# V rows of an expert lookup gathered six quarter units behind its U rows in place of eight

## The reference

```python
def peer_ffn(h, w_q, sub_keys, u_tab, v_tab):
    ...
    expert = ia * PEER_NKEYS + ib          # 8 heads x 16 experts for each token
    gate = jax.nn.softmax(best, axis=-1)
    ...
        act = jax.nn.gelu(jnp.einsum('td,thkd->thk', hb, u_tab[eb]))
        return jnp.einsum('thk,thkd->td', gb * act, v_tab[eb])
```

## Time and profile before

| what | value |
|---|---|
| median of 3 runs | 1819.41 us (1817.88 to 6214.62) |
| the profiled execution's own time | 1814.91 us |
| its span, first to last instruction | 1813.0 us |
| PE busy | 1250.6 us, 69% of the span |
| DVE busy | 1109.7 us, 61% |
| POOL busy | 1087.9 us, 60% |
| ACT busy | 255.4 us, 14% |
| gathers (queue q0) | 550.65 MB, 77.7% of 16 DMA engines' span |

### The profile page before, as it was taken

The page is one execution under the profiler, slowest core; times in us unless marked ns, Lnnn a source line. Parts: engine busy times, 40 slices in busy tenths (PEclk is TensorE's granted clock), DMA queues, the critical chain, the costliest instruction groups (busy, mean ns, idle before and its releaser), DMA issues.

```text
span 1813.0 us, 19530 instructions
## 1 busy us (share of the span) xinstructions
PE 1250.6 (69%) x7073; PEld 642.1 (35%) x7073; DVE 1109.7 (61%) x2615; ACT 255.4 (14%) x491; POOL 1087.9 (60%) x1066
## 2 busy tenths in 40 slices
PE   5999998985878577556877755465446556555487
PEld 3558676772544233112444411121112112111122
DVE  5015341677666677678666766776777777766613
ACT  2015511220111000110111200000010000100011
POOL 1111000157767777767777777777777777777764
PEclk8999989998989899778999967877886788778899
DMA  9434545799999999999999999999999999999996
GB/s 332 129 108 157 164 148 187 280 329 367 404 406 405 396 401 407 391 385 398 405 406 407 407 398 400 406 407 400 405 407 402 405 401 408 410 409 409 408 356 256
DMA packets 196409, 639.21 MB, mean 353 GB/s; under 512 B 21872, under 2 KB 23204, under 8 KB 196186
## 3 DMA queue, kind: packets, MB, share of 16 engines
q0 software_dynamic: 154992, 550.65, 77.7%
q1 hardware_dynamic: 41322, 87.31, 13.6%
HBM read 634.09 MB, written 3.59 MB: 352 GB/s over the span
## 4 chain that ended last, share of the span: by engine, by line
POOL 44%; PE 21%; DMA 16%; issue 15%; DVE 2%; ACT 1%; SPq 0%; DVEq 0%; POOLq 0%; PEldq 0%; ACTq 0%
POOL arena L564 44%; DMA arena<-in_peer_v,arena 12%; PE psum L1285 7%; PE psum L1625 4%; PE psum L1354 4%; DMA arena<-in_peer_u,arena 2%; DMA arena<-in_w_ada 1%; PE psum L1303 1%; PE psum L1637 1%; DMA arena<-in_w_in 1%; ACT arena L619 1%; DVE arena L1180 1%; DMA arena<-in_x_sample 0%; PE psum L1671 0%; PE psum L1311 0%
## 5 line engine op out<-in xcount | busy, mean ns | idle before, releaser
L1625 PE MATMUL psum<-arena 64*64 64x512 f32 x4096 | 640.3, 769 | 504.5 <-DMA arena<-in_peer_v,arena 482.2
L1180 DVE CUSTOM_DVE_ANT_0 arena<-arena 128x1024 f32<-128x1024 f32 x520 | 636.2, 1228 | 405.0 <-DMA arena<-in_peer_u,arena 389.0
L564 POOL DMA_INDIRECT arena<-in_peer_u,arena x520 | 541.1, 1041 | 222.7 <-issue 155.2
L564 POOL DMA_INDIRECT arena<-in_peer_v,arena x520 | 521.1, 1002 | 203.1 <-issue 145.8
L1625 PEld LDWEIGHTS psum<-arena 64*64 64x64 f32 x4096 | 200.0, 172 | 918.9 <-issue 808.8
L1285 PE MATMUL psum<-arena 128*128 128x264 f32 (+2 forms) x1592 | 365.4, 386 | 8.1 <-DMA arena<-in_w_branch_pool 6.3
L1285 PEld LDWEIGHTS psum<-arena 128*128 128x128 f32 x1592 | 296.2, 192 | 89.7 <-issue 37.0
L619 ACT ACTIVATE arena<-psum 128x512 f32<-128x512 f32 (+7 forms) x218 | 88.6, 446 | 481.3 <-PE psum L1285 313.1
L778 ACT ACTIVATE arena<-arena 128x16 f32<-128x16 f32 x32 | 6.9, 217 | 817.2 <-DVE arena L1180 817.2
L1354 PE MATMUL psum<-arena 128*128 128x512 f32 (+1 forms) x192 | 72.1, 536 | 4.3 <-DMA arena<-in_w_in 4.3
L1354 PEld LDWEIGHTS psum<-arena 128*128 128x128 f32 x192 | 37.0, 194 | 39.2 <-issue 32.6
(11 more groups left out here) (207 smaller groups left out, 762.5 us busy)
## 6 DMA issues: line engine op xcount, KB each, us to landing
arena<-in_w_ada SPq DMA_DIRECT2D x12, 2048.0 KB, 13.2
arena<-in_w_in SPq DMA_DIRECT2D x10, 2048.0 KB, 15.3
arena<-in_peer_wq SPq DMA_DIRECT2D x8, 2048.0 KB, 16.4
arena<-in_peer_u,arena POOLq DMA_INDIRECT x520
arena<-in_peer_v,arena POOLq DMA_INDIRECT x520, 7.6
arena<-in_w_out SPq DMA_DIRECT2D x4, 2048.0 KB, 16.9
arena<-in_w_branch_attn SPq DMA_DIRECT2D x4, 1024.0 KB, 11.4
arena<-in_w_branch_pool SPq DMA_DIRECT2D x2, 2048.0 KB, 13.9
```

What stands on the lines that cost most here:

```text
L564: pool.indirect_dma_start(out=rows_to, out_offset=None, in_=table[0], in_offset=bass.IndirectOffsetOnAxis(ap=index, axis=0)).then_inc(land ...
L1180: dve.tensor_tensor_reduce(rows_r, rows_r, h, 1.0, 0.0, ALU.mult, ALU.add, total).then_inc(u_used, 1)
L1625: ins = pe.matmul(psum[i * HW:(i + 1) * HW, sums_bank(b) + 2 * g + h, :], diags[n % 4][ps, q % 2 * GS + k + i, :], v_rows[v_buf[r]][ps, h ...
```

## The change

V is gathered and combined six quarters behind U in place of eight. What was placed by the step is put so that it keeps its place either to the V quarter or to the step:

- POOL: V(0) goes out after U(5); in step k from 6 on V(k-6) comes ahead of U(k). After U(127) come V(122) to V(125), then the samples' U rows and the rest as before.
- PE: `combine` in step k takes V(k-6). The transposes for the samples keep their place ahead of V(104), and so move from step 112 to step 110. The product for `sample_turned` stays in step 128, now ahead of V(122); `pick_rows(0, 4)` stays in step 130, now ahead of V(124); `pick_rows(4, 8)` stays ahead of V(126).
- DVE: `scale_sums(0)` moves from the start of step 40 to the start of step 38, those of blocks 1 and 2 from the end of steps 74 and 106 to the end of steps 72 and 104.
- The fold of block 0 moves from step 43 to step 41. ACT's order is the same.

```diff
-AT_ROWS = 43
+AT_ROWS = 41
+LAG = 6
...
-        for p in range(2):
-            for q in range(4):
-                u_gathers(p, q)
-        for p in range(2, UNITS):
-            for q in range(4):
-                v_gathers(p - 2, q)
-                u_gathers(p, q)
-        for q in range(4):
-            v_gathers(UNITS - 2, q)
-        for q in range(2):
-            v_gathers(UNITS - 1, q)
+        for k in range(4 * UNITS):
+            if k >= LAG:
+                v_gathers(*divmod(k - LAG, 4))
+            u_gathers(*divmod(k, 4))
+        for v in range(4 * UNITS - LAG, 4 * UNITS - 2):
+            v_gathers(*divmod(v, 4))
         for q in range(4):
             u_gathers(SAMPLES_AT, q)
...
-            if p == PH + 2:
-                scale_sums(0)
...
+                if 4 * p + q == 4 * PH + LAG:
+                    scale_sums(0)
                 dots(p, q)
...
-                if q == 2 and p in (2 * PH + 2, 3 * PH + 2):
+                if q == 0 and p in (2 * PH + 2, 3 * PH + 2):
                     scale_sums(p // PH - 1)
...
-        for k in range(8, 4 * PLACES + 8):
-            p, q = divmod(k, 4)
+        for k in range(LAG, 4 * PLACES + LAG):
+            v = k - LAG
+            u, q = divmod(v, 4)
             late_products(k)
-            if (p, q) == (SAMPLES_AT - 4, 0):
+            if v == 4 * (UNITS - 6):
...
-            if (p, q) == (SAMPLES_AT, 0):
+            if v == 4 * UNITS - 6:
...
-            if (p, q) == (SAMPLES_AT, 2):
+            if v == 4 * UNITS - 4:
                 pick_rows(0, 4)
-            if (p, q) == (SAMPLES_AT + 1, 2):
+            if v == 4 * UNITS - 2:
                 pick_rows(4, S)
```

More of the change, by code:

```diff
@@ L591, in v_gathers @@
                 gather(peer_v, v_rows[v_buf[r]], r, index_of(p, r), v_landed[v_buf[r]])
-        for p in range(2):
-            for q in range(4):
-                u_gathers(p, q)
-        for p in range(2, UNITS):
-            for q in range(4):
-                v_gathers(p - 2, q)
-                u_gathers(p, q)
-        for q in range(4):
-            v_gathers(UNITS - 2, q)
-        for q in range(2):
-            v_gathers(UNITS - 1, q)
+        for k in range(4 * UNITS):
[4 more added lines that the diff above has]
+            v_gathers(*divmod(v, 4))
         for q in range(4):
             u_gathers(SAMPLES_AT, q)
[L606 to L609, removed]
+        for v in range(4 * UNITS - 2, 4 * PLACES):
+            v_gathers(*divmod(v, 4))
         pool.wait_ge(windows_stored, 16 * 6)
@@ L1690, in _ @@
                 ins.then_inc(sample_turned, 1)
-            if (p, q) == (SAMPLES_AT, 2):
+            if v == 4 * UNITS - 4:
                 pick_rows(0, 4)
-            if (p, q) == (SAMPLES_AT + 1, 2):
+            if v == 4 * UNITS - 2:
                 pick_rows(4, S)
-            if p - 2 == SAMPLES_AT:
+            if u == SAMPLES_AT:
                 combine_samples(q)
@@ L1699, in _ @@
             else:
-                combine(p - 2, q)
+                combine(u, q)
             if k in (AT_ROWS, 4 * (2 * PH + 3), 4 * (3 * PH + 3)):
-                fold(p // PH - 1)
+                fold(k // (4 * PH) - 1)
     block.__exit__(None, None, None)
```

## The result

The changed kernel takes 1829.49 us in the median of 8 runs, the kernel before 1818.89 us. The ratio is 1.0043 with an interval of 1.0027 to 1.0059: 0.43% slower, about 8 us, where 2 us less were forecast. The time itself lies in the range of 1806 to 1830, near its upper end. The profiled execution took 1827.08 us with a span of 1825.2 us, 12.2 us more than the span before.

The account below looks back on a forecast made before the run. Gathers were taken as bound by the data the DMA engines move, about 408 GB/s; -3 - 1 + 8 - 6 = -2 us took 1819.4 to 1817, with a range of 1806 to 1830 for 8 in 10.

Parts of the forecast that it names:

- Place 3: Samples' transposes: PE waits for ACT's copy, POOL blocks 10 to 11 us; +8 us, ends +5 and +12.
- Everywhere else the order within a step is unchanged: Outside the four places: PE's dense products still precede the rows gathered in that step; no term in the sum.
- the scalings keep their distance: Scalings of blocks 1 and 2 move two steps along with their sums; no term in the sum.
- place 1: The start: V gathers begin after 24 U gathers, not 32, filling POOL's waits; -3 us, ends -5 and +2.
- Place 4: The tail: V(124), not V(122), waits behind `pick_rows(0, 4)`, so POOL's 5.94 us block goes; -6 us, ends -7.5 and -3.
- most of the small losses beside it: The tail: small transfer losses beside the 5.0 us gap mostly go with it; part of the -6 us.
- Rival (c): The start gives nothing because DVE slows POOL's issue; 1820 us, chance 17%.
- Place 2: Scaling of block 0's sums, step 40 to 38, behind a shorter route part on DVE; -1 us, ends -3 and 0.
- Rival (a): Unit borders: coefficients come too late, so PE waits at every unit and POOL behind it; 1912 us, chance 3%.
- Rival (b): Start and block 0's scaling give nothing, tail gives 3, transposes' block costs 12; +9, 1828 us, chance 15%.
- Rival (e): The block at the transposes costs only the tail's gap, +5, other terms as taken; 1814 us, chance 18%.

Follow-up runs that it names:

- park_in_before: The kernel before with only the samples' transposes moved from step 112 to step 110; ratio 1.0062 to the kernel before, 11 us.
- park_off: The changed kernel with only the samples' transposes put back to step 112; ratio 0.9986 to the kernel before.
- The repeat: The changed kernel measured once more, unedited; ratio 1.0050 to the kernel before.
- scale_in_before: The kernel before with only the scalings of blocks 1 and 2 moved to steps 72 and 104; ratio 1.0026, 5 us.
- scale_late: The changed kernel with transposes back in step 112 and scalings of blocks 1 and 2 back in steps 74 and 106; ratio 0.9963, measured again 0.9962.
- tail_alone: The kernel before with only `pick_rows(0, 4)` moved from ahead of V(122) to ahead of V(124); ratio 0.9980, a gain of 3.6 us.
- start_alone: The kernel before with only the first V group's gathers issued ahead of U(6), two groups earlier; ratio 1.0020.

## Why the prediction was wrong

The forecast was -2 us; the measurement is +8 to +9. The prediction took 2% as the least that a measurement tells from no change; the intervals here are 0.14 to 0.21% to either side, so 0.4% was told. (Its slices 11 to 38 lack 131 GB/s in sum and not 132, which changes nothing.) By its steps:

- **Place 3: the mechanism was right, the term was mis-sized.** It was put at +8 with an upper end of 12; 1540 to 1640 lost 13.4 us in the trace; it is 11 us by park_in_before and 10 to 12 us by park_off. (The repeat lost 11.0 and park_in_before 12.3.) Three parts of its working were off. First, "9.2 us to its use" was taken as the time for which the queue keeps the DMA engines busy: "being moved until about 1566.5", 8.4 us after the start of the last issue at 1558.1 (by 9.2 us it would be 1567.3; the text doesn't say what it takes off). In the changed kernel the last issue began at 1572.14 and ended at 1573.07, and behind that the engines moved 2.93 x 410 + 2 x 305 + 2 x 33 = 1877 KB, 3.6 gathers: 4.6 us at the full rate, 5.5 from the start of the issue. The same sum for park_in_before, whose last issue ended at 1568.57, is 1.43 x 406 + 5 x 206 + 5 x 3 = 1626 KB, 3.1 gathers. So the time from issue to use is not the depth of the queue. Second, PE came back at 0.50 of its clock: the transposes took 1.87 us and not 1.04, and POOL was let go 4.0 us after `combine` began at 1581.82, not "1 to 2" (in the tail of the kernel before, at a clock of 1.00, `combine` began at 1750.23 and POOL was let go 2.3 us later). POOL stood 12.74 us in place of 10 to 11. These two together are the empty time: at full rate the queue was empty at 1577.7 and data flowed again from about 1587.8, which is 10.1 us in place of 5.8. Third, the refill took some 3 us and not 2: windows of 293 to 395 GB/s up to 1600 lose 1.8 us, and windows of 343 to 400 up to 1615 another 1.5.
- **"Everywhere else the order within a step is unchanged" and "the scalings keep their distance" was the step that failed outright.** The scalings kept their distance to the sums, but they now share step 4u+4 with the coefficients. The prediction put them at nothing; they cost 5 us by scale_in_before and 4 us by scale_late. The prediction weighed the slow issue of gathers beside DVE, but only at place 1.
- **Place 4: right in kind, too large.** Forecast -6, ends -7.5 and -3. The 5.94 us block and the 204 GB/s went, as said, and PE then works through both `pick_rows` and the quarters between them without a pause from 1758 to 1792, as said. The net gain is 3.6 us by tail_alone and 3.5 by the changed kernel's trace, because two gathers of 1.99 and three of 1.57 us between 1780 and 1791 cost again, where the gathers of the kernel before from 1775 to 1790 take 0.93 to 0.99; why they are long is not shown. The step "most of the small losses beside it" failed.
- **Places 1 and 2: as forecast or somewhat better.** Place 1 was put at -3; the trace has 5.0 - 1.7 = 3.3 less, with the first V gather at 401.47 where 402 was said. Over the other profiles, kernels with V eight quarters behind and the old start lose 5.4 to 6.2 us there, those with six 1.3 to 4.2. POOL waits no more for DVE between 400 and 440, as was said, but twice for PE, 0.99 and 2.15 us. Rival (c) falls: of the four gathers of V(0) in the changed kernel one took 1.97 us and three 0.93 to 0.98. Place 2 was put at -1; PE still waits 6.95 us for the scaling and POOL 2.66 behind it, yet the windows behind (795 to 805) have 351 and 380 GB/s and not 268 and 306, a loss of (57 + 28) / 408 x 5 = 1.0 us against 3.0. Over all profiles 740 to 840 loses 5.3 to 6.5 us with V eight quarters behind and 2.1 to 5.1 with six. No run changes place 1 or place 2 alone, so both rest on these comparisons.
- **Rival (a)** did not come: PE waited once for a coefficients' tile, 4.0 us (the kernel before four times, 15.3 us in sum). **Rival (b)**, only the upper end of place 3 showing (1828), was nearest to the time, but not for its reason: the start and place 2 did give. **Rival (e)**, place 3 at the 5 us of the tail's gap, falls by the 11 to 13 us.

Summed by the ratios: +11 (place 3, park_in_before) + 5 (scalings) - 4 (tail) = +12; the whole is +8 to +9, so some 3 to 4 us of gain are left for places 1 and 2, near their 3.3 and 2 in the trace. Each of these ratios has an interval of 3 to 4 us to either side, so the sum can't settle terms of this size, and it leaves out whatever 840 to 940 costs. In the prediction's own terms: its -2, with 3 more for place 3, 4 to 5 for the scalings and 2.4 less gain in the tail, comes to +7 to +8. scale_late, which keeps all the gains and has neither loss, is 7 us below the kernel before: near the forecast without its +8, which is -10, with the smaller tail.

Open: 840 to 940 lost 0.6 us in the one profile of before and 5.0 to 6.9 in all nine with V six quarters behind. But start_alone lost 6.2 there, and park_in_before, scale_in_before and tail_alone, all with eight, 2.0 to 3.4. In that stretch DVE clears a tile ahead of four dot products, and a gather of 2.49 us stands beside it in all of them; whether one or two more long ones follow varies. The means, 6.0 with six and 3.0 with eight, speak for a cost of the shorter lag, but how much belongs to the change isn't settled; it was not tried apart.

## What to carry to other kernels

When a step is moved, look at what it now shares its place with on every engine, not only at its distance to what it depends on: the scaling was still early enough, and still cost 4 to 5 us where it took the pause that DVE had between two steps. To price a block of the engine that issues transfers, start from how much data the queue still holds at the last issue (here 3.1 to 3.6 gathers) and not from the time between issue and use, and let the engine that ends the block restart at the clock that it has after its idle time (0.50 here behind 26.23 us). Of a wait of PE the buffers take the first part (13 us of PE's wait were 2 us of POOL's). A block of POOL cost nearly its full length where gathers were all that was moved (11.48 us lost 12.3, 12.74 lost 13.4, 12.71 lost 11.0), and one of 7.08 us lost nothing at 526.62, where 1.15 of the 3.22 MB moved were plain transfers, at 401 GB/s in the window shown.

## What was not expected of the hardware

- The issue of one gather took 1.04 us (U) and 1.00 us (V) on POOL in the mean of the kernel before. Beside the moved scalings, where the dot products stand 1.14 us apart, two gathers in a row took 1.94 and 1.99 us in the changed kernel (from 1508.91) and 1.94 and 1.98 us in scale_in_before (from 1170.54). Behind the scalings of the kernel before, where the dot products start 1.28 us apart, they took 0.94 to 1.12. At 408 GB/s a gather is moved in 1.28 us, so by estimate each such pair, with the 0.30 us between gathers, puts the queue some 2 x (1.96 + 0.30 - 1.28) = 2 us behind. The fourth gather of V(0) in the changed kernel, at 405.23 among dot products that start at 405.18 and 406.32, took 1.97 us. Such a dot product need not lengthen a gather, though: the third gather of V(0), at 403.99, began 0.03 us behind one and took 0.94 us. Of the four long ones in the earlier trace rows the two of 1.68 us stand behind a release by DVE, those of 1.98 and 1.86 us behind the usual 0.30 us. What lengthens them is not shown.
- Behind its wait of 26.23 us PE had a granted clock of 0.50 from 1580 to 1584, 0.53 in the window 1584 to 1586 and 1.00 in the one behind: eight transposes took 1.87 us, where the kernel before took 1.04 for them at 1567.26 at a clock of 1.00. That lengthened a block that was already on the path.
- A closer V stream can make a stall worse elsewhere: the same `pick_rows` ahead of the same V(122) held POOL for 5.94 us with eight quarters between the streams and 10.62 with six, since it then stands two steps earlier and waits for the samples' routing.
